# The first two panels of nine products (and of the very first) run side by side, slice by slice, into two PSUM banks

## The reference, cut to what matters

```python
h = rmsnorm(x, norm_mix_g[i])
y = mixer(h, ...)                 # h @ w_in, the mixer's own work, then @ w_out
x = x + y
x = x + swiglu(rmsnorm(x, norm_ffn_g[i]), f_w13[i], f_w2[i])

def rmsnorm(x, g):
    return x * lax.rsqrt(jnp.mean(x * x, axis=-1, keepdims=True) + RMS_EPS) * g
def swiglu(h, w13, w2):
    g, u = jnp.split(h @ w13, 2, axis=-1)
    return (jax.nn.silu(g) * u) @ w2
```

## Time and profile before

| | |
|---|---|
| median of 3 runs | 1950.37 us (1949.91 to 1950.62) |
| profiled execution: its own time | 1959.19 us |
| profiled execution: span from first to last instruction | 1957.4 us |
| TensorE matmul busy | 1840.1 us, 94% |
| VectorE busy | 1306.3 us, 67% |
| ScalarE busy | 962.4 us, 49% |
| GpSimd busy | 230.0 us, 12% |
| mean granted TensorE clock | 0.962 of full speed |

### The profile page before, as it was taken

One profiled execution on the slowest core, in us unless ns is written; L12 is line 12 of the kernel. 1 busy time (PEld: TensorE's weight loads), 2 busy tenths in 40 slices (PEclk: granted clock), 3 DMA queues, 4 the chain that ended last, 5 costly groups with the idle time before them and its releaser, 6 DMA issues.

```text
span 1957.4 us, 38099 instructions
## 1 busy us (share of the span) xinstructions
PE 1840.1 (94%) x13672; PEld 1692.4 (86%) x13672; DVE 1306.3 (67%) x2035; ACT 962.4 (49%) x1249; POOL 230.0 (12%) x177
## 2 busy tenths in 40 slices
PE   7999998979999999997999999999998998899997
PEld 7999997947999986557999999999995794689997
DVE  6876766588766687667766678766654374387663
ACT  4457633644675344211775344774344544347741
POOL 0030033102000300003000303001201000030012
PEclk9999999969999999999999999999997899899998
DMA  5555654511556453102556455656451250245562
GB/s 197 169 174 182 208 176 172 162 43 64 173 183 211 155 192 108 56 1 79 180 183 210 143 173 171 199 182 208 154 195 53 82 197 12 66 150 184 190 207 74
DMA packets 77810, 289.51 MB, mean 148 GB/s; under 512 B 9611, under 2 KB 11948, under 8 KB 77356
## 3 DMA queue, kind: packets, MB, share of 16 engines
q1 hardware_dynamic: 77740, 288.59, 44.8%
HBM read 287.51 MB, written 1.05 MB: 147 GB/s over the span
## 4 chain that ended last, share of the span: by engine, by line
PE 75%; DVE 12%; POOL 5%; issue 3%; ACT 2%; DMA 1%; DVEq 1%; POOLq 1%; SPq 0%; ACTq 0%
PE bank L424 20%; PE bank L422 20%; PE bank L423 20%; DVE wlo L1306 4%; POOL sumsq L1287 3%; PE bank L584 2%; POOL square L1286 2%; PE bank L628 1%; PE bank L642 1%; PE bank L687 1%; PE bank L710 1%; DMA raw<-in_w 1%; PE bank L521 1%; DVE conv_cv L1410 1%; PE bank L544 1%
## 5 line engine op out<-in xcount | busy, mean ns | idle before, releaser
L422 PE MATMUL bank<-xh,whi 128*128 128x256 f32 (+1 forms) x2896 | 825.2, 285 | 25.5 <-DVE wlo L1306 22.4
L881 ACT CAST whi<-raw 128x1024 fp32r<-128x1024 f32 (+1 forms) x490 | 539.9, 1103 | 609.6 <-PE bank L424 550.6
L423 PE MATMUL bank<-xl,whi 128*128 128x256 f32 (+1 forms) x2896 | 820.4, 283 | 0.0
L424 PE MATMUL bank<-xh,wlo 128*128 128x256 f32 (+1 forms) x2896 | 819.4, 283 | 0.0
L1306 DVE TENSOR_TENSOR wlo<-raw,whi 128x1024 fp32r<-128x1024 f32 (+1 forms) x491 | 685.8, 1402 | 11.9 <-ACT whi L881 11.8
L422 PEld LDWEIGHTS bank<-xh,whi 128*128 128x128 f32 x2896 | 552.0, 191 | 32.7 <-issue 15.2
L424 PEld LDWEIGHTS bank<-xh,wlo 128*128 128x128 f32 x2896 | 552.7, 191 | 0.0
L423 PEld LDWEIGHTS bank<-xl,whi 128*128 128x128 f32 x2896 | 548.9, 190 | 1.2 <-issue 0.5
L424 PE MATMUL bank<-ffn_hh,wlo 128*128 128x256 f32 x880 | 248.2, 282 | 0.0
L423 PE MATMUL bank<-ffn_hl,whi 128*128 128x256 f32 x880 | 247.2, 281 | 0.0
L422 PE MATMUL bank<-ffn_hh,whi 128*128 128x256 f32 x880 | 246.8, 280 | 0.0
(11 more groups left out here) (269 smaller groups left out, 2055.3 us busy)
## 6 DMA issues: line engine op xcount, KB each, us to landing
raw<-in_w SPq DMA_DIRECT2D x414, 512.0 KB, 3.5
raw<-in_w SPq DMA_DIRECT2D x80, 704.0 KB, 4.2
att_bias<-in_bias SPq DMA_DIRECT2D x1, 3072.0 KB, 10.4
hy_decay<-in_decay SPq DMA_DIRECT2D x4, 512.0 KB, 5.9
ret_tab<-in_ret_tab SPq DMA_DIRECT2D x1, 1168.0 KB, 5.8
mla_uq<-in_uq SPq DMA_DIRECT2D x1, 1152.0 KB, 6.4
x<-in_xT SPq DMA_DIRECT2D x1, 1024.0 KB, 5.8
hy_w<-in_filt_w SPq DMA_DIRECT2D x4, 256.0 KB, 4.3
```

What stands on the lines that cost most here:

```text
L422: pe.matmul(ps, whi[:, slot, wc], hi[:, k, cols], start=first, stop=False)
L423: pe.matmul(ps, whi[:, slot, wc], lo[:, k, cols], start=False, stop=False)
L424: mm = pe.matmul(ps, wlo[:, slot, wc], hi[:, k, cols], start=False, stop=last)
L881: nc.scalar.copy(whi[:, p % RING, 0:k * P], raw[:, p % RING, 0:k * P]).then_inc(panel_hi, 1)
```

## The change

At ten places the loop "panel 0, `total`, panels 1, 2, 3" becomes "panels 0 and 1 together, `total`, panels 2 and 3". `first_panels` first waits for the weights and the banks of both panels, then goes through the eight input slices: wait for the slice, three matmuls of panel 0 into its bank, three matmuls of panel 1 into the next bank. `panel_used` is signalled for both after the last slice. The number of matmuls, their operands and the order in which each bank accumulates stay as they were.

```diff
+        def first_panels(ph, hi, lo, cols, ready):
+
+            for j in range(2):
+                pe.wait_ge(panel_lo, ph.p0 + j + 1)
+                pe.wait_ge(bank_free, ph.t0 + j + 1)
+            for k in range(K8):
+                pe.wait_ge(ready[0], ready[1] + k + 1)
+                for j in range(2):
+                    slot = (ph.p0 + j) % RING
+                    ps = bank[(ph.b0 + j) % 4][:, 0:cols.stop - cols.start]
+                    wc = slice(k * P, (k + 1) * P)
+                    pe.matmul(ps, whi[:, slot, wc], hi[:, k, cols], start=k == 0, stop=False)
+                    pe.matmul(ps, whi[:, slot, wc], lo[:, k, cols], start=False, stop=False)
+                    mm = pe.matmul(ps, wlo[:, slot, wc], hi[:, k, cols], start=False, stop=k == K8 - 1)
+                    if k == K8 - 1:
+                        mm.then_inc(panel_used, 1)
...
             if norm is not None:
-                for j in range(4):
+                first_panels(ph, hi, lo, cols, ready)
+                if norm:
+                    total(norm, cols)
+                for j in range(2, 4):
                     panel(ph, 0, j, hi, lo, cols, ready)
-                    if j == 0 and norm:
-                        total(norm, cols)
```

More of the change, by code:

```diff
@@ L481, in head_sums @@
                           stop=True).then_inc(na["sums"], 1)
[L483 to L488, removed]
+            first_panels(ph, xh, xl, A, (x_lo, C * norm))
+            total(norm, A)
+            for j in range(2, 4):
+                panel(ph, 0, j, xh, xl, A, None)
+                head_sums(None, j - 2, j - 2)
             with pe.Fori(1, 4) as i:
@@ L649, in retention_in @@
             ph = PH["in_ret"]
[L650 to L653, removed]
+            first_panels(ph, xh, xl, A, (x_lo, C * norm))
+            total(norm, B)
+            for j in range(2, 4):
+                panel(ph, 0, j, xh, xl, A, None)
             with pe.Fori(1, 4) as i:
```

## The result

| | before | changed |
|---|---|---|
| median | 1950.5 us (6 runs, 1948.1 to 1956.2) | 1983.2 us (6 runs, 1975.8 to 1984.5) |
| ratio | | 1.0157, 95% interval 1.0136 to 1.0177 |
| span of the profiled execution, mean clock | 1957.4 us, 0.962 | 1979.7 us, 0.955 |

The account below looks back on a forecast made before the run. The prediction took TensorE's stream of matmuls as the bound, so reordering touches only its holes. Later chain starts (6.6 + 6.1 us) and clock drops (12.0) made 24.7 us: 1950.4 + 24.7 = 1975 us, range 1961 to 1981.

Parts of the forecast that it names:

- The chain: Nine places behind a residual: `total`, root, `rinv`, read-out, `wlo` of panel 3 start later, costing 6.6 plus 6.1 us.
- the 0.91 of slack at three places: Three up products: panel 3 started 0.91 us after its `wlo` chain ended, absorbing that much of the 1.77 us delay.
- the 12.7 of the forecast: Nine places: 12.7 us for the later start of `total` and panel 3 alone, without any clock loss.
- Rival A: Before panel 3: holes vanish and nothing replaces them; 21 us faster, 1929 us; chance 0.04.
- The clock: New holes of some 3.5 us before panel 3, one more in layer 0: eight clock drops at 1.5 us, 12.0 us.
- the row at 709.6: Profile of before: low stretch after the idle from 706.2, nearly all worked in; basis for 1.5 us per drop.
- the two holes of layer 0's: Layer 0's up product: 2.8 us before the pair until `wlo` of panel 1, and some 3.5 us before panel 3.
- The nine waits for GpSimd and five for `xl` gone: Sign: TensorE's waits of `total` for GpSimd's sum, 13.3 us, and for `xl` slices, 2.8 us, disappear.
- nine late panels 3: Sign: at nine places panel 3 waits about 3.5 us for `wlo`, still 6.8 us after `total`.
- five new waits of 1.4 to 3.0 us in front of the up products: Sign: five further TensorE waits for `wlo` of panel 1, forecast at 1.2 to 2.8 us.
- the mean clock below 0.962: Sign, whole profile: mean clock falls below 0.962, with a low stretch behind most of the nine holes.
- Rival C: All places: two hidden clock drops count too, ten at 1.65 us; 29 us slower, 1979 us; chance 0.08.

Follow-up runs that it names:

- experiment 4: Changed kernel with 28 unused matmuls filling the hole between panels 2 and 3 at the nine places: 1962.1 us, ratio 1.0056 to the kernel before.
- experiment 2: Kernel before with only `total` moved behind panel 1, panels 0 and 1 still one after the other: 1970.0 us, ratio 1.0094.
- experiment 3: Changed kernel with `total` issued inside the pair of panels 0 and 1, after slice 5 of both: 1961.2 us, ratio 1.0048.
- experiment 10: Changed kernel without the wait for both weights, slice 7 of both panels last, `total` inside when GpSimd's sum is ready: 1950.3 us, ratio 0.9997.
- experiment 6: Changed kernel with VectorE forming `wlo` of panel 3 ahead of the norm: 1935.6 us, ratio 0.9916 to the kernel before.
- experiment 1: The kernel before run again without any edit: 1952.0 us, ratio 1.0000; its profiled execution spans 1951.7 us.
- experiment 9: Changed kernel without the wait for both weights: slices 0 to 6 of each panel, slice 7 of both, then `total`: 1968.0 us, ratio 1.0075.
- experiment 5: Kernel before with VectorE forming `wlo` of panel 3 ahead of the norm at the nine places: 1930.9 us, ratio 0.9892.
- experiment 7: Changed kernel with `wlo` of panel 3 ahead of the norm and `total` after slice 5 of the pair: 1932.4 us, ratio 0.9909.
- experiment 8: Changed kernel with pairs kept only behind down products and in the first product, up products as before: 1960.1 us, ratio 1.0050.

## Why the prediction was right in kind and short in size

**The chain, right.** Forecast were 1.77 us later for `total` behind a K8 product and 1.66 behind a down product, with 6.86 and 7.53 us from there to panel 3. Measured from the rows above: 5.89 - 3.96 = 1.93 and 5.62 - 4.02 = 1.60, with 6.76 and 702.12 - 694.70 = 7.42. Panel 3 is thus 1.83 and 1.49 us later, less the 0.91 of slack at three places: 4 x 1.49 + 2 x 1.83 + 3 x 0.92 = 12.4 us against the 12.7 of the forecast, and 11 us left in experiment 4 when the clock is taken out. Experiments 2, 3 and 10 give the loss as `total` is moved to and fro, and 6 shows what it hangs on. Rival A, which ends on the faster side, falls with 10: even without a single new wait ahead of `total` the time doesn't move.

**The clock, mis-sized.** The failing term is "8 x 1.5 = 12.0 us". The holes came as forecast, 3.3 us each at the up products. But of the price I took one low stretch of some 3.4 us a hole, 1.65 at most, from the row at 709.6. In the changed kernel's profile the granted clock stayed low for about twice as long behind six of the nine holes, as in the window from 507.40 above. These windows are layer 3's up product, with the short kind, and the whole low stretch in the second block's in product, with the long kind:

```profile
1236.40:1240.30 3.90, 3.83 (x19) 3.83 (x20) 3.71 (x7) 2.04 (x4) 0.00 (x0) 0.56 0.47 159
...
1428.00:1434.80 6.80, 5.39 (x25) 5.39 (x26) 4.28 (x6) 0.00 (x0) 0.00 (x0) 0.50 0.61 243
```

Behind a hole the long kind costs panel 3 alone 5.3 - 2.84 = 2.5 us. Five of the six fall on the path: 5 x 2.5, with 1.65 for layer 3's up product and 2 x 1.5 for the two holes of layer 0's, makes 17 us in that execution. Experiment 4, with 0.0157 - 0.0056 over several executions, makes it 20. 12.4 and 17 to 20 give 29 to 32 us, and 30.6 were measured. That the sum comes so near is partly luck, as the next paragraph shows. The bound was wrong too: I held one low stretch for the most that a hole can bring, and the range ended at 1981.

**Where the profile alone misled.** Layer 2's in product should have been 1.66 us late in all. Its panel 3 was 1.5 us late, but in the profile of before TensorE stood 3.5 us for a load in the same product (the hole at 706.2); in the changed kernel TensorE came later to that point and didn't wait there at all. By the table above, layer 2 was 4.8 us shorter than before, so that place cost less than nothing. All the rest lost 27.1 us, near the terms without layer 2's share: 12.4 - 1.5 + 17 = 28. The two make the 22.3 us between the profiles. Against experiment 1, a more usual execution of before, layer 2 won back 4.9 us and the second block lost 9.4 in place of 4.4, at a clock of 0.89 in place of 0.93: two things that were in no sum, and that nearly cancel.

**The other steps.** The nine waits for GpSimd and five for `xl` gone, nine late panels 3, five new waits of 1.4 to 3.0 us in front of the up products, the mean clock below 0.962: all as written. At eight places the hole in front of panel 3 ends with `wlo`, 3.3 us long at six of them and 4.0 and 4.1 at the in products of layers 2 and 3. Layer 1's in product had a hole of 2.8 us in place of 3.5, ended by a head sum that waited for ScalarE's `att_sq` (L968), and no low stretch behind it. Rival C, which put 29 us on the change, came nearest in size, though by ten drops of 1.65 and not by fewer and longer ones.

**Left open.** Experiments 2 and 9 say that holding TensorE costs 12 to 16 us, of which five to seven are shift. The remainder isn't shown to be the price of two holes in a row: in the profile of experiment 9 nothing holds TensorE in front of the pair, and the low stretch is still of the long kind at three of the five up products, as many as in the changed kernel. Some 6 us of it lie in the second block (348.8 us in experiment 2 and 348.2 in 9 against 354.7, at a clock of 0.92 in place of 0.89). Filling the first of the two holes wasn't tried, nor were the changed kernel and experiments 2, 4, 6 and 9 run beside each other.

## What to carry to other kernels

When a wait on an engine is filled with later work, ask what stands behind the waiting instruction on the other engines: here a small matmul fed root, reciprocal, read-out and the next weights, and delaying it by 1.6 to 1.9 us at nine places cost 31 us net, although 16 us of idle were saved. Shorten or reorder the chain first (one VectorE instruction moved gave 1.1%), then fill the holes; without the shorter chain the same filling gave nothing. Price a new hole on TensorE by the work that runs at half clock behind it, with the longest low stretch seen behind such a hole as the bound. Take the profile of one execution as one draw of the clock, and compare two profiles stretch by stretch before a difference is put down to the edit: here the second block's stretch moved by up to 21 us between kernels, most of it with the clock.

## What was not expected of the hardware

A hole of 3.3 us was followed by a low clock of 3.4 us at two of the up products and of 6.8 us at the three others, in one execution and with the same instructions around it. Executions of one unchanged kernel spread over 12 us (1946.7 to 1958.6 for before, beside experiments 5 to 8), the shortest at a mean clock of 0.969 and the longest at 0.963. And 252 matmuls whose results nobody reads took 1.01% off the changed kernel.
